# Six groups of expert activations weighed early, 384 dense columns, and a fifth batch of gathered rows, in an encoder step on one Trainium2 core

## The reference

```python
e = jnp.take_along_axis(cidx, pos, axis=-1)
gate = jax.nn.softmax(sc, axis=-1)
u = jnp.take(u_tab, e, axis=0).astype(jnp.float32)
act = jax.nn.gelu(jnp.einsum('tpkd,td->tpk', u, hb.astype(jnp.float32)), approximate=False)
vv = jnp.take(v_tab, e, axis=0).astype(jnp.float32)
return jnp.einsum('tpk,tpkd->td', gate * act, vv).astype(h.dtype)
```

## Time and profile before

| | us |
|---|---|
| median of 3 runs | 2100.55 |
| lowest, highest | 2098.74, 2101.66 |
| the profiled execution, its own time | 2100.14 |
| its span, first to last instruction | 2098.3 |
| PE busy | 2010.6 (96%) |
| DVE busy | 1333.7 (64%) |
| POOL busy | 1053.5 (50%) |
| ACT busy | 795.9 (38%) |

### The profile page before, as it was taken

One profiled execution on the slowest core, in us unless ns is written; L12 is line 12 of the kernel. 1 busy time (PEld: TensorE's weight loads), 2 busy tenths in 40 slices (PEclk: granted clock), 3 DMA queues, 4 the chain that ended last, 5 costly groups with the idle time before them and its releaser, 6 DMA issues.

```text
span 2098.3 us, 38564 instructions
## 1 busy us (share of the span) xinstructions
PE 2010.6 (96%) x13924; PEld 1959.6 (93%) x13924; DVE 1333.7 (64%) x2431; ACT 795.9 (38%) x1337; POOL 1053.5 (50%) x861
## 2 busy tenths in 40 slices
PE   5999997987999999999999999999999999999998
PEld 4898896987998899999999999999999999999997
DVE  6443444433379779899999932122368788887864
ACT  5334434422333543443444433333333333333332
POOL 3222122412332677678778877820367676765300
PEclk9999998998999999999999999999999999999997
DMA  5644622221165244444444344443879999999971
GB/s 194 193 147 131 192 92 78 73 71 57 61 201 170 80 134 129 137 135 130 135 136 131 133 138 129 134 140 130 306 241 357 338 364 350 360 346 361 333 264 43
DMA packets 185568, 381.70 MB, mean 182 GB/s; under 512 B 33792, under 2 KB 103584, under 8 KB 185376
## 3 DMA queue, kind: packets, MB, share of 16 engines
q1 hardware_dynamic: 146592, 313.30, 44.0%
q0 software_dynamic: 38912, 67.66, 9.3%
HBM read 310.44 MB, written 70.21 MB: 181 GB/s over the span
## 4 chain that ended last, share of the span: by engine, by line
PE 92%; DVE 3%; ACT 2%; issue 1%; DMA 1%; POOL 0%; DVEq 0%; SPq 0%; ACTq 0%
PE bank L887 28%; PE bank L889 28%; PE bank L888 27%; PE bank L960 1%; PE bank L1268 1%; PE bank L1169 1%; PE bank L951 1%; PE bank L1197 1%; DVE rmo L1934 1%; PE bank L1005 1%; PE bank L974 1%; DMA wring<-in_v 0%; DVE sq_sum L1783 0%; DVE mixedT L1812 0%; PE bank L1335 0%
## 5 line engine op out<-in xcount | busy, mean ns | idle before, releaser
L887 PE MATMUL bank<-h_hi,u_hi 128*128 128x272 f32 x3136 | 915.8, 292 | 33.0 <-DVE h_lo L1806 8.8
L889 PE MATMUL bank<-h_hi,u_lo 128*128 128x272 f32 x3136 | 911.3, 291 | 0.0
L888 PE MATMUL bank<-h_lo,u_hi 128*128 128x272 f32 x3136 | 905.8, 289 | 0.0
L887 PEld LDWEIGHTS bank<-h_hi,u_hi 128*128 128x128 f32 x3136 | 594.6, 190 | 41.8 <-issue 15.2
L888 PEld LDWEIGHTS bank<-h_lo,u_hi 128*128 128x128 f32 x3136 | 595.2, 190 | 0.6
L889 PEld LDWEIGHTS bank<-h_hi,u_lo 128*128 128x128 f32 x3136 | 593.6, 189 | 0.0
L800 POOL DMA_INDIRECT scratch_gates<-total,gidx x416 | 477.8, 1149 | 126.0 <-issue 125.7
L2057 DVE TENSOR_TENSOR u_lo<-wring,u_hi 128x1024 fp32r<-128x1024 f32 x252 | 307.5, 1221 | 207.7 <-ACT u_hi L1659 204.7
L720 POOL TENSOR_TENSOR u_lo<-wring,u_hi 128x1024 fp32r<-128x1024 f32 x72 | 178.5, 2479 | 486.1 <-ACT u_hi L1392 401.4
L1659 ACT ACTIVATE u_hi<-wring 128x1024 fp32r<-128x1024 f32 x271 | 286.2, 1056 | 357.2 <-PE bank L889 336.5
L887 PE MATMUL bank<-w_hi,u_hi 128*128 128x416 f32 x1016 | 358.7, 353 | 0.0
(11 more groups left out here) (278 smaller groups left out, 1760.0 us busy)
## 6 DMA issues: line engine op xcount, KB each, us to landing
wring<-in_u SPq DMA_DIRECT2D x128, 512.0 KB, 3.9
wring<-in_v SPq DMA_DIRECT2D x128, 512.0 KB, 5.5
scratch_act<-actb SPq DMA_DIRECT2D x128, 272.0 KB, 2.1
scratch_gates<-zeros SPq DMA_DIRECT2D x64, 416.0 KB, 5.0
a<-scratch_act SPq DMA_DIRECT2D x32, 832.0 KB, 7.7
g<-scratch_gates SPq DMA_DIRECT2D x32, 832.0 KB, 10.5
wring<-in_w_in SPq DMA_DIRECT2D x28, 512.0 KB, 4.7
wring<-in_w_x SPq DMA_DIRECT2D x24, 512.0 KB, 4.2
```

The costliest lines, as they stand in the source:

```text
L887: pe.matmul(out, whi, xhi, start=first, stop=False)
L888: pe.matmul(out, whi, xlo, start=False, stop=False)
L889: return pe.matmul(out, wlo, xhi, start=False, stop=last)
```

## The change

The change is in the expert layer. Line numbers of the kernel after are other ones (its row gather is at L850, its activation gather at L858, its row adds at L2276).

1. `ND` falls from 416 to 384: three whole token tiles. The 32 tokens that leave the dense part become a fifth gathered batch: `NB` = 5, 160 rows and 160 gathers of activations. The fourth tile needs no packing any more, `pack` goes, and 8 x 48 = 384 scatters are left.
2. The activations of the last six groups (`WEIGHED` = 6, from group `W0` = 26) are multiplied by their gates inside the first product, three blocks after the block itself (`weigh` on DVE), before SP stores them (`weighed_tile` waits for `w_made`). SP loads their gates one group ahead, behind the wait for `scattered`, which so stands in group 25 and no longer in group 31.
3. The second product takes these six groups first: group 31 straight from `actb`, then 26 to 30 (their activations loaded again, no gates, no multiply), then 0 to 25 as before.
4. The row buffers move to a place that is free before the first product ends, and are `VROWS` = 6. POOL gathers the first six rows as soon as the lists are there, without a wait for PE.
5. Rows are due from block 13 on, 109/160 blocks apart. Behind the 32 activations of batch 0, POOL gathers one and two activations in turn before a row.

The core of the diff:

```diff
-ND = 416
+ND = 384
...
+WEIGHED = 6
+W0 = KEYS // GROUP - WEIGHED
...
-VROWS = 4
+VROWS = 6
 NROWS = NB * STEPS
-ROW_FROM = 14
-ROW_EVERY = (KEYS - 10 - ROW_FROM) / NROWS
+ROW_FROM = 13
+ROW_EVERY = (KEYS - 6 - ROW_FROM) / NROWS
...
+            def weighed_tile(g, j, table, nxt):
+
+                made_low(g, j, False)
+                sp.sem_inc(passed, 1)
+                weights(j, table[nxt, j])
+                sp.wait_ge(w_made, (g - W0) * GROUP + j + 1)
+                sp.dma_start(d["act"][g, j], actb[:, j]).then_inc(act_stored[j], 16)
+
             for j in range(GROUP):
-                first_tile(last, j, d["v"], 0, False)
+                first_tile(W0 - 1, j, d["u"], W0, False)
+                if j == 1:
+                    for t in range(NTD):
+                        sp.wait_ge(scattered[t], 16 * PH * TOPK)
+                    load_gates(W0)
+            for g in range(W0, last + 1):
+                for j in range(GROUP):
+                    weighed_tile(g, j, d["u"] if g < last else d["v"], g + 1 if g < last else last)
+                    if j == 1:
+                        if g < last:
+                            load_gates(g + 1)
+                        if W0 < g <= W0 + 2:
+                            for k in range(GROUP):
+                                sp.wait_ge(act_stored[k], 16 + 16 * g)
+                            load_acts(g - 1, (g - 1 - W0) % 2)
...
             pool.wait_ge(shuf_landed, 16 * KG * 3 * NB)
-            pool.wait_ge(unit_done, 4 + 2 * (NPQ + KEYS))
             for n in range(VROWS):
                 gather_row(n)
...
             for n in range(VROWS, NROWS):
-                if cells:
-                    gather_activation(*cells.pop(0))
+                for _ in range(1 + n % 2):
+                    if cells:
+                        gather_activation(*cells.pop(0))
                 gather_row(n)
...
+            def weigh(n):
+
+                g, j = n // GROUP, n % GROUP
+                dve.wait_ge(gu_landed[g % 2], 16 * ((g - W0) // 2) + 16)
+                dve.wait_ge(unit_taken, 2 * n + (4 + 2 * NPQ + 2))
+                dve.tensor_tensor(actb[:, j, 0:ND], actb[:, j, 0:ND], gring[g % 2][:, j], ALU.mult).then_inc(w_made, 1)
+
+            for n in range(W0 * GROUP, KEYS):
+                low(n, n % GROUP)
+                if n >= W0 * GROUP + RING - 1:
+                    weigh(n - (RING - 1))
...
             def weights_of(x):
 
-                g, j = x // GROUP, x % GROUP
-                if j == 0:
-                    dve.wait_ge(ag_landed[g % 2], 32 * (g // 2) + 32)
-                dve.tensor_tensor(wf[:, j % 2], aring[g % 2][:, j], gring[g % 2][:, j], ALU.mult).then_inc(wf_ready, 1)
+                q, j, p = x // GROUP, x % GROUP, (x // GROUP - 1) % 2
+                if q == 0:
+                    if j < RING - 1:
+                        weigh(KEYS - (RING - 1) + j)
+                    src = actb[:, j, 0:ND]
+                elif q < WEIGHED:
+                    dve.wait_ge(ag_landed[p], 16 * ((q - 1) // 2) + 16)
+                    src = aring[p][:, j]
+                else:
+                    if j == 0:
+                        dve.wait_ge(ag_landed[p], 32 * ((q - WEIGHED) // 2) + (32 + 16 * ((WEIGHED - p) // 2)))
+                    src = wf[:, j % 2]
+                    dve.tensor_tensor(src, aring[p][:, j], gring[p][:, j], ALU.mult).then_inc(wf_ready, 1)
                 low(KEYS + x, j)
                 dve.wait_ge(whi_ready, x + 1)
-                dve.tensor_tensor(w_lo[:, j], wf[:, j % 2], w_hi[:, j, 0:ND].bitcast(F32), ALU.subtract).then_inc(w_ready, 1)
+                dve.tensor_tensor(w_lo[:, j], src, w_hi[:, j, 0:ND].bitcast(F32), ALU.subtract).then_inc(w_ready, 1)
```

More of the change, by code:

```diff
@@ L97 @@
 NG = TS
-ND = 416
+ND = 384
+NTD = ND // P
 NCHUNK = ND // CTOK
[L100 to L105, removed]
+BATCH_OF = tuple((0, row) for row in range(0, P, NG)) + ((1, 0),)
+NB = len(BATCH_OF)
+SPARSE = ((slice(0, P), NT - 2, 0), (slice(0, NG), NT - 1, 1))
 U1_GROUPS = 1
@@ L319, in encoder_step @@
         same = ret.place("same", [P, TOPK * (PH - 1) * TOPK])
-        more = ret.place("more", [P, NT - 1, TOPK])
+        more = ret.place("more", [P, NTD, TOPK])
         scr = ret.place("scr", [P, TOPK * TOPK])
@@ L367, in encoder_step @@
         wf = late.place("wf", [P, 2, ND])
-        assert late.end <= late_at + 56 * 1024
+        assert late.end <= picked.start_of["es"]
         table_of_gates = d["gates"].rearrange("c p g k -> (c p g k)")
@@ L691, in second_tiles, with group_at @@
+            def second_tiles(q, nxt):
+                for j in range(GROUP):
+                    sp.wait_ge(low_ready, q * GROUP + (KEYS + j + 1 - POOL_TILES))
                     sp.sem_inc(passed, 1)
                     weights(j, d["v"][nxt, j])
+            def group_at(q):
+                return last if q == 0 else W0 + q - 1 if q < WEIGHED else q - WEIGHED
+            for q in range(WEIGHED):
+                second_tiles(q, group_at(q + 1))
+                if q == 0:
+                    for j in range(GROUP):
+                        sp.wait_ge(act_stored[j], 16 + 16 * (KEYS // GROUP))
+                if q:
+                    sp.wait_ge(w_ready, q * GROUP + GROUP)
+                    if q + 2 < WEIGHED:
+                        load_acts(group_at(q + 2), (q + 1) % 2)
+                    else:
+                        load_group(group_at(q + 2), (q + 1) % 2)
@@ L699, in reload_group @@
                 load_group(g, p)
[L701 to L705, removed]
+            with sp.Fori(0, W0 // 2 - 1) as i:
+                for r in range(2):
+                    second_tiles(i * 2 + (WEIGHED + r), i * 2 + (r + 1))
+                    reload_group(i * 2 + r, i * 2 + (r + 2), (r + 1) % 2)
+            second_tiles(last - 1, W0 - 1)
             for c in range(0, C, 2):
@@ L1741, in w_high, with w_high_made @@
             def w_high(x, s, p):
-                act.wait_ge(wf_ready, x + 1)
+                act.wait_ge(wf_ready, x + (1 - WEIGHED * GROUP))
                 act.activation(w_hi[:, s, 0:ND], wf[:, p], ACT.Copy).then_inc(whi_ready, 1)
+            def w_high_made(x):
+                q, j = x // GROUP, x % GROUP
+                if q == 0:
+                    act.wait_ge(w_made, (WEIGHED - 1) * GROUP + j + 1)
+                else:
+                    act.wait_ge(ag_landed[(q - 1) % 2], 16 * ((q - 1) // 2) + 16)
+                src = actb[:, j, 0:ND] if q == 0 else aring[(q - 1) % 2][:, j]
+                act.activation(w_hi[:, j, 0:ND], src, ACT.Copy).then_inc(whi_ready, 1)
             g = KEYS // GROUP - 1
```

107 lines of the change are left out of this document (50 added, 57 removed).

## The result

The kernel after takes 2133.53 us in the median of four runs (2129.61 to 2136.28), the kernel before, run beside it, 2099.72 (2098.74 to 2101.66): a ratio of 1.0157, with a 95% interval of 1.0144 to 1.017. The forecast was 2140, slower with a chance of 0.85. The profiled execution took 2135.25 us, its span is 2133.5.

The account below looks back on a forecast made before the run. PE, busy for 96% of the span, was taken as the bound. Terms of -43.0, -1.0, +78, +4 and +2.3 summed to +40, taking the span from 2098.3 to 2138.6 and the time to 2140 us; range 2100 to 2190.

Parts of the forecast that it names:

- PE's width: Both products: matmuls of 384 instead of 416 columns take 4.193 us per block, 0.337 us less for 127 blocks; -43.0 us.
- Rival (e): Matmuls of 384 columns do not follow the straight line through 272 and 416; moves 43 us by a few; no chance given.
- Change-over: Start of the second product: PE's 0.95 us standstill goes because activation and gate loads are spread over the first product; -1.0 us.
- First product: Early multiplies, SP's earlier wait for scatters and the first six row fetches do not reach PE; 0 us.
- POOL: Second product, blocks 13 to 76: 2.5 gathers per row at 1.57 us are slower than PE's pace, so PE waits; +78 us.
- Rival (a): Gathers on POOL cost near their floor of 1.25 us, the stall falls to nothing, 2060 us; chance 0.11.
- point of decision: Gather time on POOL at which the kernel would show no change: 1.38 us.
- Rival (b): POOL is starved further by longer unbroken DVE work: gathers at 1.82 us, stall 131 us, time 2193 us; chance 0.09.
- Behind block 76: Late second product: DVE at 3.88 of 4.193 us per block and DMA at 402 GB/s both just fit; +4 us.
- rival (c): DMA is a lower ceiling, 358 GB/s: blocks behind 76 take 0.52 us more, 24 us in all, 2160 us; chance 0.09.
- Folding: Folding takes 32 products instead of 24, which took 6.98 us; +2.3 us.
- Rival (d): PE's pauses while POOL is late lower its clock; it hides, or costs 162 us at half speed; chance 0.03.

Follow-up runs that it names:

- the version at two paces: Kernel after with one activation per row, six activations ahead, rows due 0.74 block apart up to row 120, 0.58 behind; 2061.0 us, ratio 0.9818.
- the profiled runs with 1.304 and 1.441: Kernel after with row adds of 64 columns for 1024: 1.441 us per gather, 2112.77 us; with low halves of 128 columns too: 1.304, median 2079.0 us.
- the version with short row adds and short low halves: Kernel after with row adds of 64 columns and second-product low halves of 128 columns, both in place of 1024; 2079.0 us, ratio 0.9899.

## Why the prediction was right, term by term

**The sum** was +40 on the span, the span gave +35.2. The mechanism, the place and the order of the waits came as predicted; the sizes of the terms were off both ways. POOL's term was 6 us too large and the one behind block 76 was 7 us too small, so that the sum came within 5 us is in part luck.

**PE's width**, predicted -43.0: the table's stretches give -28.9 to block 76 at 4.16 us, -16.2 to block 120 and -1.5 twice behind it, -48, of which 1 is the change-over's idle time. The line through 272 and 416 columns gave 4.193 us per block, and 4.16 was measured; 0.033 us for 127 blocks is the 4 us of difference. Rival (e) came true in its size, a few us off the line, but towards narrower blocks.

**Change-over**, -1.0: the idle 0.95 us of the earlier trace rows is gone, and the opening block takes 4.7 us where it took 6.1. That T is 1.3 us earlier says nothing: in the kernel after and its nine versions here it lies between 1488.4 and 1491.3.

**First product**, 0: it cost nothing that T shows, but the step behind it was mis-sized. The last scatter was to start at about 1283 and started at 1317.4:

```profile
L824 POOL DMA_INDIRECT scratch_gates<-total,gidx x384: 954/959/2677, 690.6 to 1317.4; - x192
...
  DVEq L2179: 52.1, 4
```

POOL had 64 to 75 us less to do, as worked out, but waited 52.1 us for DVE to finish a head's gates, where the kernel before had waited 13.7. The estimate took POOL's work off its end as if nothing else fed it. SP passed its wait and issued the first load of gates at 1332.7, so 15 us of cover were left of 50.

**POOL**, +78, measured 71.7, by the same chain. The first activation came at T + 5.1 (predicted +8), the next 32 at 1.380 us each (1.474), the 212 behind at 1.548 (1.57), the last was through at about T + 379 (+390), and block 76 began some nine and a half behind that (seven). Two steps of these seven were short. The row was to land after the shortest time of the earlier trace rows, 4.3 us; row 90, gathered at 1864.46, was added at 1872.20, 7.7 us later, near the median of 7.5. And row 91 is due behind block 75 too (13 + 91 x 109/160 = 74.99): it was gathered behind the last activation and added at 1873.59, ahead of block 76. The first 32 gathers were faster beside a DVE that was busy for 40% and not 54% of that stretch. POOL's waits on acc were to be far below 114.6 us; they were 80.0, none of it in the paced stretch. For the rest, the line through 54% and 81% of DVE overstated the slope: the version at two paces kept 1.567 with DVE at 90% (268.91 of 300). The 1.657 and 1.82 of the earlier trace rows were means over seven and seventeen gathers, too few. Rival (a), gathers near 1.25, needed a DVE with little to do: 1.304 came only with DVE at 36% (86.33 of 240). Its point of decision holds, though: the profiled runs with 1.304 and 1.441 took 2083.26 and 2112.77 us, and the straight line between them passes 2100 at 1.38, as worked out. Rival (b), 1.82, fell.

**Behind block 76**, +4, measured 193.9 - 44 x 4.16 = +10.9. This is the term that was most wrong for its size. The sum weighed a steady demand of 402 GB/s against single slices near 400, and took nothing for the burst with which a stall ends. 6.5 of the 10.9 us lie in blocks 76 to 79, which took 23.2 us for 16.6. As soon as the activations are used up POOL makes up rows, seven from 1867.32 to 1876.00, and the activations and gates of a group are loaded in the same moment (SP, 1870.57 and 1871.13). ACT then waits 9.3 us for a v block, until 1892.22; PE stands still for 3.0 us behind block 78, and blocks 76 and 79, each behind a pause, take 5.84 us (1880:1900 above: PE 17.0 of 20 us, granted clock 0.89). In the version with short row adds and short low halves, whose DVE has little to do, PE pauses behind block 78 too, for 7.0 us, and blocks 76 to 79 hold all 10 us that it loses up to block 120. So DVE isn't what holds the block up; that the rows and loads ahead of it are is read from this order of starts, and no run separates them.

The steady demand itself just fits, as predicted. DMA in 1880:2080 of the kernel after, in 40 slices:

```profile
GB/s 407 401 409 386 404 377 327 383 408 410 383 404 402 311 391 407 410 381 406 380 378 397 406 408 381 408 371 364 401 410 407 384 405 412 393 395 408 393 260 205
```

Slices reach 412, and the mean of the first 38 is 392. The version without gathers of later activations asks for the same 402 from block 24 on, gets 394 in 1560:1880 and has lost 5 us by block 120. The version at two paces asks for 0.52 + 0.52 / 0.74 + 0.39 MB per block of 4.16 us, about 389 GB/s, and gets it. So rival (c) had the right place, but not its ceiling of 358, which would have cost 24 us. The Trainium skill, page DMA: Bandwidth & Descriptors (Where 436 GB/s comes from), puts about 358 GB/s as what HBM gives one core; its page HBM Reference (Specifications (TRN2)) says that a core that streams alone gets well above its share, and the 386 to 389 GB/s over 400 us of the version at two paces agree with the second. No run here has a second core.

**Folding**, +2.3, measured 9.0 us against 7.0, +2.0.

**Rival (d)**, PE's clock, was seen: 0.91 over the paced stretch, 0.83 in 1720:1740, where PE's pauses sent it to its lower level, 1.2 GHz, for part of the time. It is why one sign came out too small: PE was to wait 70 to 90 us for w_lo and waited 48.3, since slower blocks made up the other 23. Up to block 76 it hid, as predicted: POOL's pace set block 76 to nine to eleven us behind the last activation in four kernels whose granted clocks in 1610:1850 were 0.91, 0.91, 0.92 and 0.96. Behind it, where POOL no longer paced, blocks 76 and 79 cost 1.7 us each.

What the prediction did not see is that the loss lies in the order alone. It named the slope, 3.93 us of POOL per row against 2.86, and not that one gather less per two rows would take the loss from 72 us (at block 76) to 44 (at block 120), and that a due time that POOL can keep would take away nearly all of it.

## What to carry to other kernels

Where one queue issues for several deadlines, divide the time that the order gives it by the instructions that it must issue in it, stage by stage, and compare with their measured pitch from start to start; the busy share over the span doesn't show it. A due time written into program order is a wait for everything behind it, so set it to the pace of the slowest supplier, and let the end be denser: here that turned 1.6% slower into 1.8% faster with the same work. A stall also ends with a burst: what was held back is issued at once, and a mean demand doesn't show what queues behind it.

## What the runs showed of the hardware that was not expected

An indirect gather of 128 indices costs POOL 1.25 us from start to start when DVE's instructions are short, for 4 KB rows and single numbers alike (means of 972 and 980 ns), and 1.5 to 1.6 us beside DVE's long ones, and hardly more when DVE goes from 70% busy (1.548) to 90% (1.567). The core's DMA engines carried 386 to 389 GB/s for 400 us beside a PE that was busy for 399.9 of them, and 394 GB/s for 320 us in the version without gathers of later activations.
